# Two transformer blocks on one core: two norms from one weighted sum, key scores a tile later, a finish by halves

## What is computed

```python
def rms_norm(x, g): return x * rsqrt(mean(x*x, -1) + 1e-6) * g

# first block
h = x
h = h + 0.5 * swiglu(rms_norm(h, ln_ffn1), w1_gate, w1_up, w1_down)      # width 2816
h = h + mixer(rms_norm(h, ln_mix) @ w_in) @ w_out                         # gated recurrence + attention
h = h + 0.5 * swiglu(rms_norm(h, ln_ffn2), w2_gate, w2_up, w2_down)
gate = sigmoid(rms_norm(h, ln_ple) @ w_ple_gate)
h = h + gate * (p @ w_ple_proj)
x = rms_norm(h, ln_final)                                                 # output of block one

# second block
sh1, sc1, gt1, sh2, sc2, gt2 = split(c @ w_mod + b_mod, 6)
z = (rms_norm(x, norm1_g) * (1 + sc1) + sh1) @ w_in
y = g_a * pool_mixer(z) + g_b * forgetting_attention(z)
x = x + gt1 * (y @ w_out)
h2 = rms_norm(x, norm2_g) * (1 + sc2) + sh2
# product keys: 8 heads, 2 x 128 keys, top 16 pairs per head and token of 16384 experts
x = x + gt2 * sum_k gelu(h2 . u[k]) * gate[k] * v[k]
return rms_norm(x, final_g)
```

## Time and profile before

| | |
|---|---|
| median of 3 runs | 1628.04 us (1626.09 to 1629.92) |
| profiled execution | 1627.11 us, its span 1625.3 us |
| busy: TensorE, VectorE, ScalarE, GpSimd | 87%, 61%, 34%, 44% of the span |
| mean granted TensorE clock | 0.959 of full speed |
| HBM read | 424.9 MB |
| of that, expert rows | 268.5 MB |

### The profile page before, as it was taken

The page is one execution under the profiler, slowest core; times in us unless marked ns, Lnnn a source line. Parts: engine busy times, 40 slices in busy tenths (PEclk is TensorE's granted clock), DMA queues, the critical chain, the costliest instruction groups (busy, mean ns, idle before and its releaser), DMA issues.

```text
span 1625.3 us, 21353 instructions
## 1 busy us (share of the span) xinstructions
PE 1420.8 (87%) x8186; PEld 1086.8 (67%) x8186; DVE 989.0 (61%) x1779; ACT 556.8 (34%) x936; POOL 711.1 (44%) x442
## 2 busy tenths in 40 slices
PE   8999899998999899999999888778777777777886
PEld 8999899978999898899888773333333333333332
DVE  5788423555786624622543648777777777777653
ACT  4434345424444334544343432222222222222211
POOL 2434346402344444396575466444434443444430
PEclk9999999999999999999999999999999999899988
DMA  7776554303577453143333369999999999999993
GB/s 312 262 265 218 184 181 151 104 27 126 210 260 257 162 201 114 63 163 131 104 105 130 121 230 413 420 420 421 420 421 420 421 420 420 420 421 420 420 420 134
DMA packets 59206, 427.16 MB, mean 263 GB/s; under 512 B 6576, under 2 KB 6896, under 8 KB 7792
## 3 DMA queue, kind: packets, MB, share of 16 engines
q0 software_dynamic: 36864, 268.45, 39.9%
q1 hardware_dynamic: 20736, 149.96, 26.1%
q10 hardware_dynamic: 1520, 7.60, 1.2%
HBM read 424.93 MB, written 1.05 MB: 262 GB/s over the span
## 4 chain that ended last, share of the span: by engine, by line
PE 38%; DMA 28%; DVE 15%; issue 8%; POOL 5%; ACT 5%; ACTq 0%; DVEq 0%; POOLq 0%; SPq 0%
DMA keys<-in_expert_uv,arena 21%; PE ps L413 6%; PE ps L418 6%; PE ps L414 5%; DMA rows_x<-in_expert_uv,arena 5%; POOL wlo L319 5%; PE ps L834 4%; PE ps L835 4%; PE ps L488 2%; PE ps L490 2%; PE ps L489 2%; DMA ring<-in_w 2%; DVE arena L1274 2%; DVE arena L1589 2%; ACT whi L901 1%
## 5 line engine op out<-in xcount | busy, mean ns | idle before, releaser
L319 POOL TENSOR_TENSOR wlo<-ring,whi 128x1024 fp32r<-128x1024 f32 x162 | 409.9, 2539 | 513.0 <-ACT whi L901 512.6
L413 PE MATMUL ps<-nh,whi 128*128 128x256 f32 x1440 | 364.9, 290 | 11.8 <-ACT nh L915 6.0
L901 ACT ACTIVATE whi<-ring 128x1024 fp32r<-128x1024 f32 x236 | 243.8, 1054 | 355.1 <-PE ps L418 163.5
L414 PE MATMUL ps<-nh,wlo 128*128 128x256 f32 x1440 | 356.7, 284 | 0.0
L413 PEld LDWEIGHTS ps<-nh,whi 128*128 128x128 f32 x1440 | 277.4, 193 | 18.0 <-issue 5.9
L414 PEld LDWEIGHTS ps<-nh,wlo 128*128 128x128 f32 x1440 | 278.0, 193 | 0.3
L418 PE MATMUL ps<-nl,whi 128*128 128x256 f32 x1440 | 207.1, 286 | 0.0
L319 DVE TENSOR_TENSOR wlo<-ring,whi 128x1024 fp32r<-128x1024 f32 x74 | 106.8, 1454 | 138.3 <-ACT whi L901 132.6
L418 PEld LDWEIGHTS ps<-nl,whi 128*128 128x128 f32 x1440 | 188.4, 193 | 2.5 <-DVE nl L1221 0.5
L1712 POOL DMA_INDIRECT arena<-in_expert_uv,arena x96 | 109.5, 1140 | 152.9 <-PE ps L835 139.8
L1589 DVE CUSTOM_DVE_ANT_0 arena<-arena 128x1024 f32<-128x1024 f32 x96 | 122.4, 1275 | 44.7 <-DMA arena<-in_expert_uv,arena 40.6
(11 more groups left out here) (303 smaller groups left out, 2383.4 us busy)
## 6 DMA issues: line engine op xcount, KB each, us to landing
ring<-in_w SPq DMA_DIRECT2D x118, 1024.0 KB, 4.9
arena<-in_wmod SPq DMA_DIRECT2D x24, 1024.0 KB, 5.0
small<-in_small ACTq DMA_DIRECT2D x1, 2816.0 KB, 19.6
arena<-in_expert_uv,arena POOLq DMA_INDIRECT x96, 26.5
h<-in_x ACTq DMA_DIRECT2D x1, 1024.0 KB, 8.0
keys<-in_keys ACTq DMA_DIRECT2D x1, 1024.0 KB, 26.1
rows_w<-in_expert_uv,arena POOLq DMA_INDIRECT x64, 25.5
out<-h SPq DMA_DIRECT2D x2, 512.0 KB
```

The costliest lines, as they stand in the source:

```text
L319: return v.tensor_tensor(wlo[:, tile % TILES, :], ring[:, tile // 2 % RAW, at:at + TILE], whi[:, tile % TILES, :].bitcast(F32), ALU.subtract)
L413: mm(to, hi[:, k, :], nh[:, k, :], start=(k == 0), stop=False)
L414: mm(to, lo[:, k, :], nh[:, k, :], start=False, stop=False)
L901: fn(whi[:, tile % TILES, :], ring[:, slot % RAW, at:at + TILE], ACT.Copy).then_inc(S("high_w"), 1)
```

## The change

1. *First norm.* A root of `eps` at the very start loads the square-root table. The sums wait for x alone (the constants `con` have a semaphore of their own). The angles, sines and lower bounds of the gates move behind VectorE's first and second weighted sum and ScalarE's second gate. Six loads of small operands (5.5 MB) are issued behind the first norm's rounding. Fillers: 26 and 12 instead of 44 and 24.
2. *Modulation halves.* The last two weighted sums of each SwiGLU are done in halves behind down products 0 to 3; the second `modulation` moves from down product 2 to 6.
3. *Norms 4 and 5 in one.* One sum of squares weighted with gain squared (plus eps) gives norm 5 of norm 4's output without forming it. A plain sum beside it (PSUM bank 7, squares in `ga`) gives norm 4, applied to `h` later. ScalarE rounds with the shift as bias straight to `nh`; `low_shifted` does the low part with the shift in one step; the shift of `sq` follows behind. The forget product moves behind projection slot 1, ScalarE's exponential and logarithm behind slot 2. The same form of shift is used at norm 6 (now 5).
4. *Key scores.* `key_scores(hd - 1)` stands between the two tiles of slot `S_PQ + hd` from head 2 on, score 0 ahead of the turns, score 7 at the end.
5. *Finish.* The last unit's last four rows are handled one by one; total, squares and scaling go by halves of 512 columns; the last half is scaled by ScalarE and stored from its own queue.

```diff
+def pick_groups(j):
+    sizes = [GROUP] * (GROUPS - 1) + ([1] * SINGLES if j == UNITS - 1 else [GROUP])
+    return [(q, sum(sizes[:q]), size) for q, size in enumerate(sizes)]
 ...
@@ tensor: features(n, turn=0, split_at=None, between=None)
                     last.then_inc(S("tiles_done"), 1)
+                    if between and t == 0:
+                        between()
@@ tensor: swiglu
-                    if j in (0, 2):
-                        modulation(mod + (turns - 1) * MOD_RING + j)
+                    if j == 0:
+                        modulation(mod + (turns - 1) * MOD_RING)
+                    if j == 6:
+                        modulation(mod + turns * MOD_RING)
@@ tensor: residual, with plain=True in the embedding stage
+            def plain_sum(c):
+                pe.wait_ge(S("plain_squared"), c + 1)
+                last = mm(ps[:, 7, 0:T], ones[:, :], ga[:, c, :], start=(c == 0), stop=(c == C - 1))
 ...
@@ tensor: start
             pe.wait_ge(S("constants"), 2)
-            keep_busy(44, bank=5)
-            pe.wait_ge(S("vec_landed"), 32)
+            keep_busy(26, bank=5)
             for c in range(C):
                 square_sum(0, c)
-            keep_busy(24, bank=5)
+            keep_busy(12, bank=5)
@@ tensor: queries
             features(S_PQ, split_at=7)
+            key_scores(0)
             for n in range(4):
                 turn_around(sq, n)
-            key_scores(0)
             for hd in range(1, PH):
-                features(S_PQ + hd)
+                features(S_PQ + hd, between=(lambda: key_scores(hd - 1)) if hd >= 2 else None)
 ...
-                key_scores(hd)
+            key_scores(PH - 1)
@@ scalar: shift
-            def shift(m, first):
+            def shift(k, first):
                 for c in range(C):
-                    act.wait_ge(S("scaled"), (m - 5) * C + c + 1)
-                    fn(sq[:, c, :], sq[:, c, :], ACT.Identity, bias=mod[:, first + c:first + c + 1]
-                       ).then_inc(S("shifted"), 1)
-                    if c:
-                        act.wait_ge(S("shifted"), (m - 5) * C + c)
-                        high_x(c - 1)
-                act.wait_ge(S("shifted"), (m - 4) * C)
-                high_x(C - 1)
+                    act.wait_ge(S("scaled"), k * C + c + 1)
+                    fn(nh[:, c, :], sq[:, c, :], ACT.Identity, bias=mod[:, first + c:first + c + 1]
+                       ).then_inc(S("high_x"), 1)
+                act.wait_ge(S("low_x"), (6 + 2 * k) * C)
+                for c in range(C):
+                    fn(sq[:, c, :], sq[:, c, :], ACT.Identity, bias=mod[:, first + c:first + c + 1]
+                       ).then_inc(S("shifted"), 1)
@@ scalar: swiglu
                 gate(n + 2, 1, before)
+                if before == 0:
+                    bounds_and_sines()
                 tile -= 8
                 with act.Fori(1, turns) as i:
@@ vector: swiglu, half_residual
                     weighted(mod + b, pairs)
+                    if mod == 0:
+                        (angles, bounds)[b]()
 ...
-                for b in range(2):
-                    weighted(mod + 2 * turns + b, turns + pairs)
 ...
+                    if j < 4:
+                        weighted(mod + 2 * turns + j // 2, turns + mod // 2, part=j % 2)
@@ vector: block two
-            norm(4, V("final1", 0, C), h, "block1_out")
-            modulated_norm(5, V("norm1", 0, C), C)
-            low_x(5)
+            modulated_norm(4, V("norm1", 0, C), C, V("final1", 0, C))
+            low_shifted(5, 0)
+            dve.wait_ge(S("plain_std"), 1)
+            own(v.reciprocal(rstd[:, 1, :], std[:, 1, :]))
+            for c in range(C):
+                ins = v.scalar_tensor_tensor(h[:, c, :], h[:, c, :], V("final1", c), rstd[:, 1, :], ALU.mult, ALU.mult)
```

More of the change, by code:

```diff
@@ L726, in _ @@
                         step(base + j)
+                    if base == S_IN2 and j == 1:
+                        forget()
             def fa_score(group):
@@ L966, in _ @@
             root(1)
+            act.wait_ge(S("gain_squared"), 1)
+            own(fn(coef[:, 3 * C:4 * C], coef[:, 2 * C:3 * C], ACT.Sqrt, bias=eps[:, 0:1]))
             high_norm(1)
@@ L1065, in _ @@
                 if j:
-                    square(4, 2 * j - 2)
-                    square(4, 2 * j - 1)
+                    for c in (2 * j - 2, 2 * j - 1):
+                        square(4, c)
+                    for c in (2 * j - 2, 2 * j - 1):
+                        plain_square(c)
             square(4, C - 2)
             square(4, C - 1)
+            plain_square(C - 2)
+            plain_square(C - 1)
             root(4)
-            for c in range(C):
-                square(5, c)
-            root(5)
-            shift(5, 0)
-            act.wait_ge(S("decay_abs"), 1)
-            own(fn(fl[0:96, 1, :], fl[0:96, 1, :], ACT.Exp))
-            fn(fl[0:96, 1, :], fl[0:96, 1, :], ACT.Ln, bias=1.0).then_inc(S("decay_log"), 1)
+            act.wait_ge(S("plain_summed"), 1)
+            fn(std[:, 1, :], ps[:, 7, 0:T], ACT.Sqrt, bias=eps[:, 0:1], scale=1.0 / D).then_inc(S("plain_std"), 1)
+            shift(0, 0)
             act.wait_ge(S("padded"), 1)
@@ L1113, in _ @@
             for c in range(C):
-                square(6, c)
-            root(6)
-            shift(6, 3 * C)
+                square(5, c)
+            root(5)
+            shift(1, 3 * C)
             act.dma_start(fgrow, a["final_g"].partition_broadcast(P).rearrange("p a t -> p (a t)")
@@ L1173, in _ @@
             for j in range(UNITS):
-                for q in range(GROUPS):
-                    activate(j, q)
+                for q, first, size in pick_groups(j):
+                    activate(j, q, first, size)
                 if j + AHEAD < UNITS:
@@ new lines, in bounds @@
+            def bounds():
+                dve.wait_ge(S("sines"), 1)
+                own(v.tensor_tensor(ang[:, 2, :], cos[:, :], cos[:, :], ALU.mult))
+                own(v.tensor_scalar(cos[:, :], ang[:, 2, :], -2.0, 1.0, ALU.mult, ALU.add))
+                dve.wait_ge(S("lb_exp"), 1)
+                own(v.tensor_tensor(lb[:, 4, :], lb[:, 2, :], lb[:, 3, :], ALU.add))
+                own(v.reciprocal(lb[:, 5, :], lb[:, 4, :]))
+                own(v.tensor_tensor(lb[:, 0, :], lb[:, 2, :], lb[:, 5, :], ALU.mult))
+                own(v.tensor_scalar(lb[:, 1, :], lb[:, 0, :], -1.0, 1.0, ALU.mult, ALU.add))
@@ L1301, in _, with half_residual @@
             swiglu(S_FFN1, 0, 0)
-            def half_residual(slot):
+            def half_residual(slot, mod):
+                turns = FB // 2
                 for j in range(C):
@@ L1581, in choose, with dots @@
                     choose_experts(j)
-            def dots(j, q):
+            def dots(j, first, size):
                 u = unit(j)
-                for k in range(q * GROUP, (q + 1) * GROUP):
+                for k in range(first, first + size):
                     g = j * TK + k
```

265 lines of the change are left out of this document (164 added, 101 removed).

## The result

The changed kernel takes 1609.01 us (median of 4 runs, 1606.51 to 1612.58), the kernel before 1627.80 beside it; the ratio is 0.9886, with a 95% interval of 0.9868 to 0.9905. The forecast was 1592.4 with a range of 1583 to 1606. The direction was right, the gain about half of it: 18.8 us on the medians, where 34.7 were forecast.

What follows compares the result with a forecast made beforehand. TensorE's chain up to its last projection tile, then a DMA-bound gather stage of 634.1 us and a 21 us tail, set the time. Gains 4.0 + 7.9 + 5.9 + 9.4 + 7.5 = 34.7 from 1627.1 gave 1592.4 us, range 1583 to 1606.

Steps and rivals of the forecast that it cites:

- What bounds the kernel: Whole kernel: the end is TensorE's last projection tile, plus 634.1 us of DMA-bound gathers, plus a 21 us tail.
- Item 1: Start, first norm: first matmul 9.2 us earlier, part given back; 4.0 gained, from 9.2 gained to 5.4 lost.
- (a): First SwiGLU: angles, taken as 3.9 us, precede tile 8's low part; tile 8 at 48.7, 5.8 of 9.2 left.
- Item 2: Modulation halves, down products of both SwiGLUs: waits at the second product go; 7.9 us gained, from 4.8 to 7.9.
- (b): First SwiGLU: lower-bound work delays tile 12's low part to about 61, wanted at 60.2; costs 1.0 us.
- (c): First SwiGLU's loop: two table loads in each of 4 turns, 10.2 us of ScalarE; charged 0.8, bounds 0 and 10.2.
- The earlier wait at 168 to 170: First SwiGLU: wait for a weight load that SyncE queues behind a modulation load; claimed to stay.
- Item 3: Norms 4 and 5 in one sum: tile 0 ends 11.9 us earlier, part given back; 5.9 gained, bounds 3 and 8.
- Item 4: Second shift and key scores in the query heads: 9.4 us gained, bounds 6 and 11; 6.8 us per head.
- The rival in which GpSimd binds the heads: Query heads: GpSimd's low parts stretch to 2.9, a head takes 7.5, 4 us return; 1596.4 us, chance 0.15.
- Item 5: Tail: last four rows weighed singly and finish by halves; 7.5 us gained, bounds 5 and 8.5.
- the first rival: First SwiGLU's loop: table loads bind, two thirds of 10.2 us pass through, item 1 loses 2; 1598.4 us, chance 0.20.

Runs made afterwards that it cites:

- e14: The kernel before with only SyncE's queue changed: three ring slots issued ahead of the modulation's last slot in both SwiGLUs; 1618.20 us.
- e3: The changed kernel with the six deferred loads issued behind the loop of the first SwiGLU; 1599.71 us.
- e4: The changed kernel with angles, sines, exponentials and bounds moved from the first two gates into the first down product, loads unmoved; 1603.60 us.
- e1: The changed kernel with the start of the kernel before, all else changed; 1602.30 us.
- e2: The changed kernel plus one SiLU activation of one column behind the sines, so the loop is entered with the SiLU table; 1607.73 us.
- e5: e4 with the six deferred loads issued behind ScalarE's third square of the first down product; 1599.19 us.
- e8: e5 with the last unit's rows in groups of 4, 4 and eight singles instead of 4, 4, 4 and four singles; 1599.72 us.
- e11: The changed kernel with only SyncE's queue changed: three ring slots issued ahead of the modulation's last slot in both SwiGLUs; 1597.99 us.
- e15: e11 with the modulation's last two weighted sums whole ahead of each down product; 1605.64 us.
- e6: e5 with the modulation's last two weighted sums whole ahead of each down product; 1606.41 us.
- e12: e8 with e11's queue order and the even tiles' low parts of the second layer's third product group on VectorE instead of GpSimd; 1584.42 us.
- e16: e13 with ScalarE's exponentials and sines behind the second norm's roundings instead of in the down product; 1578.93 us.
- e13: e12 with only two of the six loads in the down product, the rest in the mixer, and bounds behind the second norm's low parts; 1581.29 us.

## Why the prediction was wrong, point by point

**What bounds the kernel: right.** Last projection tile to last dot took 636.1 us (forecast 634), and what was saved ahead of it came off the whole, but for 2 us. These 2 us are no scatter: the distance is 633.8 and 634.1 in the traces of e14 and of the kernel before, and 635.4 to 636.4 in the sixteen of kernels with the change. No run shows their cause.

**Item 1, first norm: this step failed.** The gain was 9.3 at the first matmul as forecast, but the sum in (a), "tile 8 at 48.7, against 54.49. Of the 9.2, 5.8 are left", is wrong by 7.5 us. Its terms: the angles taken as 3.9 were 7.9 (47.13 to 55.00), since two of them fell beside low parts of GpSimd. The rows behind the 3.9 had a sign of it: there only the first and smallest of the eleven, of 128 x 4 elements, stood beside a low part, and it took 1.83 us instead of 0.16 and ended with it, at 17.02. And the weighted sum started 3.6 late: tile 6's slot was requested 1.0 later than rolled and landed after 9.9 us, where 7 to 8 had been taken, beside the deferred loads. (e3 gets 8.1 back at tile 8, e4 6.1.) The two make the 7.5, as near as the rows tell. A term was missing as well: behind the wait of 8.33 TensorE ran at the lower clock (0.54 from 50 to 60). I had rows 9 for just this and used them in item 2 alone; a wait of 6 was in the forecast, with no stretch of lower clock behind it. As a whole the new start lost 6.7 on the medians (e1), beyond the item's poor end of 5.4 lost, where 4.0 gained was forecast; part of this loss was paid at the queue, which comes next. Term (b) is lost in this; (c), 0.8 for the loop's table loads, is not contradicted: e2 took them away for 1.3, inside the scatter.

**The loop's slack, and the wait at 170.** "The earlier wait at 168 to 170, for a weight load that SyncE queues behind a modulation load, stays": it did not stay, it grew, from 2.24 to 3.57, with 0.53 of the clock behind it. I had seen the mechanism and priced it as a constant. The time at which VectorE ends the last sum of the loop, which the queue waits for, does not set it: it is 168.33 in the kernel after and 149.67 in e5, and the waits are 3.57 and 3.63. What goes with the wait is the lead: the modulation load goes out 1.6 us ahead of the first down product in all of these and in the kernel before, but 3.8 us ahead in e3 and e4, and there the wait is gone with the old order too. At the same 1.6 the ring slot behind it lands in 8.3 to 8.4 us with the new start (the kernel after, e2, e5, e8) and in 6.9 with the old (e1, wait 2.15); why is open. Counted from the start of the first down product, the other order is worth 9.0 us at norm 1 to the kernel after (e11) and 5.2 to the one before (e14).

**Item 2, modulation halves: right.** e15 is 7.65 above e11 and e6 7.2 above e5; forecast 7.9. The wait at the second down product is gone in both SwiGLUs, as was said it would be. (By its 22 k-tiles each, the place so called is the third product of the eight.)

**Item 3, norms in one sum: mechanism right, size off.** 2.3 us were gained of 5.9 (bounds 3 and 8). From the embedding product to tile 0's end it took 14.5 us instead of 26.1, 11.6 less (forecast 12). But "the decay chain ... lies beside projections ... its rows end ten later" held nothing for GpSimd: the rows end 18.4 later (721.3 against 702.9), and they stretch four low parts to 4.4, as before, but at a place where TensorE has no room left for it: a wait of 3.63 instead of 1.44, and 0.84 of the clock. e12 gives 3.4 back, which makes 5.7.

**Item 4, key scores: right, a little low.** Last norm to the last tile took 62.7 us instead of 74.4: 11.7 gained, 9.4 forecast, with 6.65 us in most heads (forecast 6.8). One part had no term: before, TensorE had 0.50 of the clock from 901.0 to 907.8, in the first tiles of the queries, and after 1.00. The rival in which GpSimd binds the heads did not happen; its mechanism did happen, one stage earlier.

**Item 5, tail: 5.3 of 7.5.** The four singles follow without a pause, but the group ahead of them starts behind a wait of 2.81 at 2.07 us for two matmuls instead of 1.02, so TensorE's backlog ends 7.9 behind the start of the last dot (1601.79 + 1.02 against 1594.96). e8, without that group, takes 1.5 off. The size is of these two traces: the distance is 18.0 and 16.3 with the old tail (before, e14) and 11.3 to 14.7 with the new one.

**The rivals.** I gave 0.20 to the loop's table loads and nothing to the queue. The end of the range was too near: the first rival with the poor ends of items 3 and 4 makes 1604.7, not 1606; item 1's own poor end, 5.4 lost, in its place makes 1608.1, and no poor end of the clock was added to either. The measured 1609.0 lies beyond all three. No chance was given to waits that cost twice, though rows 9 showed it. Of the signs of being wrong, one came: a wait of 2.07 in the first loop, at 132.44; it is not in e2, and its cause is open.

## What to carry to other kernels

When work is moved off the critical path, price it beside what runs on the other engines at its new place, not where it stood. Count every new wait of TensorE with a stretch of lower clock behind it, as a range from several rows, since one and the same wait cost an estimated 1.6 us more in one trace and 4.2 in another. And for each queue that carries two streams, ask at its last turn which one stands behind the other's wait: here the other order was worth 9.5 us before the change and 11 after it.

## What the runs showed of the hardware

- A stretch at the lower clock lay behind waits of 8.33, 2.07 and 3.57 us in the first SwiGLU (windows at 0.54, 0.83 and 0.53), also where TensorE had been busy without a break ahead. Waits of 0.6 to 1.1 (e16) had none. For one wait of 3.6 the clock of the next 10 us was 0.84 in one trace (e5) and 0.54 in another (e8); for one of 3.35 it was 1.00, 0.84 and 0.71 (e12, e16, e13).
- Single operations of VectorE on 64 x 256 elements take 0.28 to 0.35 us alone and 2.40 to 2.54 while GpSimd does a low part of 128 x 1024 (2.35): one that meets a low part ends up to 0.2 us behind it. In e3 another one was hit (2.56 at 43.11, GpSimd from 43.05 to 45.39), and a weighted sum of seven steps took 5.79 instead of 3.61. GpSimd's low part takes 2.4 alone and 4.4 beside VectorE's 32 x 2048 additions, and the additions take 4.4 instead of 2.3.
- Six DMA issues on ScalarE's queue held it for 4.4 us (18.96 to 23.4, 0.33 to 1.00 each), and its next roundings behind them.
- A weight load of 1 MB landed in 9.9 us beside the six deferred loads and in 5.0 without them (the slot of tile 6, kernel after and e3).
- A loop that is entered with another table than its own gets its table loads inside, two in each of four turns; one activation ahead of it takes them all out.
